# Building the second one-hot matrix four tokens at a time on VectorE

## The reference, cut to what matters

```python
s1 = jnp.einsum('thc,hkc->thk', q[:, :, 0], sub_keys1)
s2 = jnp.einsum('thc,hkc->thk', q[:, :, 1], sub_keys2)
...
e1 = jnp.take_along_axis(i1, ic // PEER_TOPK, axis=-1)
e2 = jnp.take_along_axis(i2, ic % PEER_TOPK, axis=-1)
idx = (e1 * N_KEYS + e2)
gate = jax.nn.softmax(vc, axis=-1)
...
pre = jnp.einsum('td,tkd->tk', xb, expert_u[ib])
a = jax.nn.gelu(pre) * gb
out = jnp.einsum('tk,tkd->td', a, expert_v[ib])
```

## Time and profile before

| | us |
|---|---|
| median of 3 runs | 3401.39 (3395.29 to 3402.13) |
| span of the profiled execution | 3398.5 |
| median of the runs less that span | 2.9 |
| TensorE busy | 3245.2 (95%) |
| VectorE busy | 2274.4 (67%) |
| GpSimd busy | 1352.5 (40%) |
| stage of the change, first to last group | 758 to 1048 |

### The profile page before, as it was taken

One profiled execution on the slowest core, in us unless ns is written; L12 is line 12 of the kernel. 1 busy time (PEld: TensorE's weight loads), 2 busy tenths in 40 slices (PEclk: granted clock), 3 DMA queues, 4 the chain that ended last, 5 costly groups with the idle time before them and its releaser, 6 DMA issues. The chain is left out here.

```text
span 3398.5 us, 51546 instructions
## 1 busy us (share of the span) xinstructions
PE 3245.2 (95%) x18667; PEld 2817.4 (83%) x18667; DVE 2274.4 (67%) x4666; ACT 1339.8 (39%) x2016; POOL 1352.5 (40%) x739
## 2 busy tenths in 40 slices
PE   8988999999999999999899999999989999999999
PEld 6756799999999999999686667788878877668877
DVE  7753888989995888887785777655460067654440
ACT  3444133335554433333313774422231145743331
POOL 3014356666665422221230664222223322444433
PEclk9989999999999999999999999999999999999999
DMA  7502457778999999998455504122212141133322
GB/s 240 147 26 106 167 162 253 238 242 306 370 354 359 391 371 361 361 364 291 137 170 131 95 2 161 63 62 62 62 46 68 46 132 57 70 105 93 94 79 93
DMA packets 235080, 588.98 MB, mean 173 GB/s; under 512 B 52580, under 2 KB 113508, under 8 KB 230797
## 3 DMA queue, kind: packets, MB, share of 16 engines
q1 hardware_dynamic: 177644, 420.58, 37.9%
q0 software_dynamic: 36864, 134.23, 10.6%
q10 hardware_dynamic: 20384, 31.73, 2.6%
HBM read 529.03 MB, written 56.91 MB: 172 GB/s over the span
## 5 line engine op out<-in xcount | busy, mean ns | idle before, releaser
L445 POOL TENSOR_TENSOR ahead_low<-w_raw,ahead_high 128x1024 fp32r<-128x1024 f32 (+1 forms) x159 | 421.3, 2650 | 872.8 <-ACT ahead_high L381 872.7
L241 PE MATMUL psum<-h_high,ahead_high 128*128 128x512 f32 (+1 forms) x1384 | 493.3, 356 | 4.7 <-POOL ahead_low L445 4.7
L242 PE MATMUL psum<-h_low,ahead_high 128*128 128x512 f32 (+1 forms) x1384 | 490.3, 354 | 0.0
L243 PE MATMUL psum<-h_high,ahead_low 128*128 128x512 f32 (+1 forms) x1384 | 488.9, 353 | 0.0
L381 ACT ACTIVATE ahead_high<-w_raw 128x1024 fp32r<-128x1024 f32 (+1 forms) x159 | 178.0, 1120 | 739.1 <-PE psum L243 701.8
L2179 POOL TENSOR_TENSOR pick_u_low<-pick_u_raw,pick_u_high 128x1024 fp32r<-128x1024 f32 x128 | 306.9, 2398 | 210.0 <-ACT pick_u_high L2302 208.9
L241 PE MATMUL psum<-peer_h_high,pick_u_high 128*128 128x384 f32 x1024 | 353.0, 345 | 9.0 <-POOL pick_u_low L2179 9.0
L242 PE MATMUL psum<-peer_h_low,pick_u_high 128*128 128x384 f32 x1024 | 346.9, 339 | 0.0
L243 PE MATMUL psum<-peer_h_high,pick_u_low 128*128 128x384 f32 x1024 | 344.0, 336 | 0.0
L241 PEld LDWEIGHTS psum<-h_high,ahead_high 128*128 128x128 f32 x1384 | 259.8, 188 | 47.0 <-issue 5.0
L243 PEld LDWEIGHTS psum<-h_high,ahead_low 128*128 128x128 f32 x1384 | 260.9, 188 | 40.4
(11 more groups left out here) (439 smaller groups left out, 8170.4 us busy)
## 6 DMA issues: line engine op xcount, KB each, us to landing
pick_u_raw<-in_expert_uT SPq DMA_DIRECT2D x128, 512.0 KB
v_raw<-in_expert_v SPq DMA_DIRECT2D x128, 512.0 KB
mod_w<-in_w_mod SPq DMA_DIRECT2D x88, 512.0 KB, 3.8
w_raw<-in_ffn_up SPq DMA_DIRECT2D x84, 512.0 KB, 3.6
gelu_dram<-pick_gelu ACTq DMA_DIRECT2D x128, 192.0 KB
gates_dram<-gate_plane SPq DMA_DIRECT2D x24, 1024.0 KB
g<-gates_dram SPq DMA_DIRECT2D x31, 768.0 KB
w_raw<-in_ffn_down SPq DMA_DIRECT2D x29, 704.0 KB, 4.1
```

The costliest lines, as they stand in the source:

```text
L241: nc.tensor.matmul(bank, w_high, x_high, start=first, stop=False)
L242: nc.tensor.matmul(bank, w_high, x_low, start=False, stop=False)
L243: return nc.tensor.matmul(bank, w_low, x_high, start=False, stop=last)
L445: nc.gpsimd.tensor_tensor(w_low[r % 2][:, :, :], raw[r % n_raw][:, :, :], w_high[r % 2][:, :, :].bitcast(F32), ALU.subtract).then_inc(k.w_ ...
```

## The change

For a group, the four combined instructions (compare, then multiply, 128 elements for one token, with the token's number and weight as per-partition scalars) go. In their place come one comparison of 512 elements, with the four tokens' second numbers broadcast along the keys, and one multiplication of 512 elements in place, with the four weights broadcast. The comparison for hot2 is issued first, then the one for hot1 as before, then a wait on V for the comparison of hot2, and the multiplication, which raises hot_ready.

```diff
-                    nc.vector.tensor_tensor(hot1[r][:, :, :], iota.unsqueeze(1).to_broadcast([P, group, N_KEYS]),
-                                            f.picks[:, 0, n].unsqueeze(2).to_broadcast([P, group, N_KEYS]), ALU.is_equal)
-                    for j in range(group):
-                        n = g * group + j
-                        ins = nc.vector.tensor_scalar(hot2[r][:, j, :], iota, f.picks[:, 1, n:n + 1], f.picks[:, 2, n:n + 1], ALU.is_equal, ALU.mult)
-                    ins.then_inc(hot_ready, 1)
+                    numbers = iota.unsqueeze(1).to_broadcast([P, group, N_KEYS])
+                    of_token = lambda i: f.picks[:, i, n].unsqueeze(2).to_broadcast([P, group, N_KEYS])
+                    nc.vector.tensor_tensor(hot2[r][:, :, :], numbers, of_token(1), ALU.is_equal).then_inc(V.sem, 1)
+                    V.n += 1
+                    nc.vector.tensor_tensor(hot1[r][:, :, :], numbers, of_token(0), ALU.is_equal)
+                    dve.wait_ge(V.sem, V.n)
+                    nc.vector.tensor_tensor(hot2[r][:, :, :], hot2[r][:, :, :], of_token(2), ALU.mult).then_inc(hot_ready, 1)
```

## The result

| | before | changed |
|---|---|---|
| median of 5 runs, us | 3397.4 (3391.9 to 3402.1) | 3409.6 (3407.5 to 3417.1) |
| ratio, 95% interval | 1 | 1.0042 (1.0027 to 1.0057) |
| span of the profiled execution, us | 3398.5 | 3412.9 |

The account below looks back on a forecast made before the run. VectorE was taken to set the stage, by 0.09 us per chunk over TensorE. 0 + 11 + 2 + 4 = +17 us on the span 3398.5 gave 3415.5, the median 3418; eighty in a hundred between 3400 and 3446.

Parts of the forecast that it names:

- VectorE's own demand falls by 0.07 us a group: On VectorE in the stage, a group takes 1.81 us instead of 1.88, 6.7 us less over 96 groups.
- The multiplication and the subtraction exclude each other: VectorE's multiplication, caught by GpSimd's subtraction of two SBUF tensors, ends 0.55 us after the subtraction does.
- 25 to 45 of 96 blocked: Of the stage's 96 multiplications on VectorE, some 25 to 45 take well above 0.69 us, held up by a subtraction.
- Weights in time: a block costs TensorE nothing; sum 0: In chunks with weights in time, blocks take only VectorE's lead; gain and loss cancel: 0, between -4 and +6 us.
- Late weights: y - 0.7 each, 11 in all: Where late weights start the subtraction y later, TensorE is pushed by y - 0.7; five stretches, 9 to 17, taken as 11 us.
- First group +2: The stage's first multiplication falls in a subtraction and ends at 762.3 instead of 760.4, with TensorE idle: +2 us.
- Clock +4: New 2 us waits on TensorE lower its granted clock two or three more times: +4 us, between 0 and +14.
- The median stands 2.9 us above the span: The runs' median was taken to lie 2.9 us above the profiled span, turning 3415.5 into 3418 us.
- R1: Rival: every block counts, subtraction and multiplication meeting at random, 40 us on VectorE; +39, 3440 us; chance 20%.
- R2: Rival: no slower, as phases settle and the slower pace lets weights land in time; 3398 to 3406 us; chance 25%.
- R3: Rival: faster, the multiplication isn't blocked and the full 4 us come back; 3397 us; chance 3%.
- R4: Rival: dearer groups, the wait ends the overlap, 2.06 us a group, 17 us on VectorE; +30, 3432 us; chance 4%.

Follow-up runs that it names:

- experiment 1: The changed kernel, with the multiplication taking the weights from a copy in PSUM instead of SBUF: 3396.4 us, ratio 1.0005 to the kernel before.
- experiment 2: The kernel before, with its hot1 comparison reading the key numbers from SBUF instead of PSUM, giving it two SBUF inputs: 3418.7 us, ratio 1.0066.
- run 7: The changed kernel with dots from the 37th on over 256 instead of 1024 elements: 3403.6 us, against 3398.7 for the kernel before with the same dots.

## Why the prediction was right

The forecast was 3418 us in 3400 to 3446, slower with 0.70; measured 3409.6, over the 3408 from which it counts as slower by less than 2. It was +17 on the profiled execution, measured +12 in the medians and +14 in the spans. The mechanism was right as well as the number: the sum was out in one term, the clock's. Step by step:

- *VectorE's own demand falls by 0.07 us a group.* Right: 1.79 us in experiment 1, where nothing blocks.
- *The multiplication and the subtraction exclude each other.* Right, and shown from both sides: without two SBUF inputs it goes (experiment 1), and an old instruction given two of them gets it (experiment 2). The end 0.55 us after the subtraction held for every block in every kernel, to 0.02.
- *25 to 45 of 96 blocked.* 23, two under the range. Seven met a subtraction that was on time, which apart from the first group's 2.0 come to 1.9 us in sum; 16 met a late subtraction, with 16 us. Each of the seven chunks with one dot was followed by a block, so the lead was taken away as worked out.
- *Weights in time: a block costs TensorE nothing; sum 0.* Right: the chunks not over 6.25 us cost 1.3 more, and run 7 has the block with no wait behind it.
- *Late weights: y - 0.7 each, 11 in all.* Right: at 829.06 y is 829.06 - 824.75 - 1.57 = 2.74, so 2.0, and TensorE waited 2.2; the chunks over 6.25 us have 10.1 in all. (The 0.7 should read 0.6: TensorE wants the second group half of 1.92 us after the first, and that is 0.96, not 1.06. The trace has 0.95. So 2.1 us were due. The 11 itself was a choice within 9 to 17, and that it came so close is in part luck.)
- *First group +2.* 1.85.
- *Clock +4.* This term was mis-sized. It took each wait of 2 us as one idle time of TensorE. But TensorE gets these 2 us in two pieces, with a group's eight matmuls between: after the first group's 4.17 us, its longest idle time in the stage is 1.11 us. The granted clock fell once in the stage, after that first wait, with no more loss than before (0.63 and 0.95 in the two windows from 762 to 770, before 0.57 and full), and not again. Before the change it fell also at 1066 to 1070, right behind a wait of 1.96 us for the low part. That wait is not there in the changed kernel, whose stage ends 13 us later, and the clock stays full:

```profile
762.00:766.00 4.00, 3.35 (x17) 3.05 (x17) 3.96 (x7) 1.07 (x1) 0.39 (x1) 0.63 0.61 180
...
1066.00:1070.00 4.00, 4.00 (x24) 4.00 (x24) 2.96 (x6) 1.54 (x3) 0.48 (x1) 1.00 0.84 260
```

The wait ahead of the fall at 1066 in the kernel before, on TensorE:

```profile
1065.10 0.44 PE L241 MATMUL psum<-peer_h_high,pick_u_high 128*128 128x384 f32 x1 [1.96 <-POOL pick_u_low L2179]
```

- *The median stands 2.9 us above the span.* It doesn't: the profiled execution of the changed kernel took 3414.7 us with a span of 3412.9, 1.8 around it, and was itself 5 over the median of its five runs. The median of before moved from 3401.4 to 3397.4 with more runs. So the median lies 3.3 us under the span instead of 2.9 over it; this and the sum's 2.6 us too much on the span make up the 8 us between forecast and median.

R1 (every block counts) had the right rule for a kernel without slack: in experiment 2, 22 us of blocks cost 21. But its 40 us of blocks came in no kernel with whole dots, and in the changed one the phases settled. R2 (no slower) failed as the late weights stayed: ScalarE's wait for the DMA sank only from 67.1 to 54.6 us. R3 (no block) fell with the 23 blocks, and R4 (dearer groups) with the 1.79 us of experiment 1. The fixed costs of the Trainium skill ("VectorE: DVE Perf Modes", errata section) gave 21 us more on VectorE without any block; the measured group is shorter than the old one, 1.79 against 1.88.

## What to carry to other kernels

Before replacing small VectorE instructions by a wide one, ask where each input lies: the combined instruction had one tensor in PSUM and two scalars, the multiplication two tensors in SBUF, and it met a GpSimd instruction with two SBUF inputs that was busy for 39% of the stage. Whether such a block costs anything is a matter of the lead that the blocked engine has over its consumer: 68 us of blocks cost 5 with slack, 22 cost 12 with little (13 against experiment 1) and 21 with none. The cure here was to keep one input in PSUM. It only gave back the loss, as TensorE's own pace was the floor already.

## What the runs showed of the hardware that was not expected

An indirect DMA on GpSimd is not quite indifferent to the multiplication. While a multiplication runs, mostly right behind a subtraction, it often takes 1.23 us or more where such a one takes 0.93 to 0.96 otherwise (33 of the 86 in the stage take over 1.05), and in the stage the mean rises from 948 to 1066 ns (91.7 us for 86; before the change 81.5 for 86). In turn 24 of the 73 unblocked multiplications take over 0.70 and up to 0.75 us instead of 0.68. Both belong to the second input in SBUF: with the weights in PSUM (experiment 1), 36 indirect DMAs of the stage run beside a multiplication, none takes over 0.96 us, and no multiplication over 0.68. GpSimd had room for its part, and no run here separates what this costs.

The exclusion also works the other way round. Once in the stage a multiplication came first, and the subtraction took 2.84 us instead of 2.40; with short dots (experiment 7) this happened five times, with up to 2.83 us. The prediction counted only the price on VectorE. In the changed kernel, the indirect DMA, then this pair:

```profile
831.61 1.23 POOL L1936 DMA_INDIRECT peer_row<-in_expert_u,row_expert  x1
...
1039.01 0.68 DVE L2458 TENSOR_TENSOR pick_hot<-pick_hot,picks 128x512 f32<-128x512 f32 x1
...
1039.12 2.84 POOL L2179 TENSOR_TENSOR pick_u_low<-pick_u_raw,pick_u_high 128x1024 fp32r<-128x1024 f32 x1 [2.28 <-ACT pick_u_high L2302]
```
